# First norm: sums of squares on TensorE, first weights split in two pieces, a third projection tile run part by part

## The reference, cut to what matters

```python
def rmsnorm(x, g):
    return x * rsqrt(mean(x * x, axis=-1) + EPS) * g          # over 1024 channels

h = rmsnorm(x, norm_mix)                                      # x: 1024 positions x 1024 channels, float32
proj = h @ w_in + b_in                                        # 5 * 1024 columns
conv_val, conv_gate, pool_in, gate_a, gate_b = split(proj)    # 1024 columns each
u = causal_dwconv(conv_val * sigmoid(conv_gate), taps=31)     # then LayerNorm, silu, @ conv_w_out
...                                                           # pooled branch, gated merge, @ mix_w_out, + x
...                                                           # x = x + gdfn(rmsnorm(x)); final rmsnorm
```

## Time and profile before

| | |
|---|---|
| median of 3 runs | 1362.0 us (1360.88 to 1363.01) |
| the profiled execution | 1359.67 us |
| its span, first to last instruction | 1357.9 us |
| TensorE busy with matmuls | 1332.1 us (98% of the span) |
| DVE / POOL / ACT busy | 853.0 / 733.3 / 392.2 us |
| mean granted TensorE clock | 0.995 |

### The profile page before, as it was taken

How to read it: one execution, slowest core, us unless ns; L and a number is a source line. 1 busy time by engine, 2 the same in 40 slices (tenths; PEclk the granted TensorE clock), 3 DMA queues, 4 the chain that set the end, 5 groups by cost and what they waited for, 6 DMA issues and landing times.

```text
span 1357.9 us, 15759 instructions
## 1 busy us (share of the span) xinstructions
PE 1332.1 (98%) x6092; PEld 1108.4 (82%) x6092; DVE 853.0 (63%) x823; ACT 392.2 (29%) x555; POOL 733.3 (54%) x486
## 2 busy tenths in 40 slices
PE   7999999999999999999999999999999999999997
PEld 6888888888888788878887788888888888888887
DVE  6799999999997545545696455544554453320225
ACT  4311221211112441111245344343443433322210
POOL 5645536554453353356967887778777714434101
PEclk9999999999999999999999999999999999999999
DMA  5111111110111112344402222212221238531003
GB/s 195 63 49 58 34 47 47 47 47 31 47 53 42 46 47 78 121 133 147 141 31 93 93 93 87 79 68 93 94 78 68 103 118 315 188 109 62 0 1 124
DMA packets 32930, 114.47 MB, mean 84 GB/s; under 512 B 3040, under 2 KB 9184, under 8 KB 28768
## 3 DMA queue, kind: packets, MB, share of 16 engines
q1 hardware_dynamic: 29328, 104.12, 22.3%
q10 hardware_dynamic: 3536, 9.44, 1.9%
HBM read 93.62 MB, written 19.92 MB: 84 GB/s over the span
## 4 chain that ended last, share of the span: by engine, by line
PE 88%; DVE 4%; POOL 2%; issue 1%; ACT 1%; DVEq 0%; POOLq 0%; ACTq 0%
PE ps L1323 29%; PE ps L1325 29%; PE ps L1324 29%; DVE ga_r L1173 1%; DVE tmp L1081 1%; POOL h_lo L496 0%; POOL w_lo L541 0%; DVE res L1300 0%; PE ps L1377 0%; POOL h_lo L541 0%; PE ps L1387 0%; DVE raw L1179 0%; DVE res L1133 0%; DVE res L1166 0%; DVE res L1168 0%
## 5 line engine op out<-in xcount | busy, mean ns | idle before, releaser
L1323 PE MATMUL ps<-h_lo,w_hi 128*128 128x512 f32 (+1 forms) x972 | 374.9, 386 | 8.8 <-DVE h_lo L944 7.3
L1325 PE MATMUL ps<-h_hi,w_hi 128*128 128x512 f32 (+1 forms) x972 | 372.0, 383 | 0.0
L1324 PE MATMUL ps<-h_hi,w_lo 128*128 128x512 f32 (+1 forms) x972 | 372.0, 383 | 0.0
L1027 DVE SCALAR_TENSOR_TENSOR ps<-tmp,par,ps 128x1024 f32<-128x1024 f32 x224 | 267.7, 1280 | 0.0
L457 POOL TENSOR_SCALAR w_hi<-raw 128x1024 fp32r<-128x1024 f32 x66 | 71.6, 1085 | 309.7 <-issue 253.0
L1323 PEld LDWEIGHTS ps<-h_lo,w_hi 128*128 128x128 f32 x972 | 183.3, 189 | 46.9 <-DVE h_lo L944 8.7
L1324 PEld LDWEIGHTS ps<-h_hi,w_lo 128*128 128x128 f32 x972 | 183.3, 189 | 35.7 <-issue 0.5
L1325 PEld LDWEIGHTS ps<-h_hi,w_hi 128*128 128x128 f32 x972 | 183.2, 188 | 35.5
L1323 PE MATMUL ps<-ga_r,w_hi 128*128 128x512 f32 (+1 forms) x428 | 166.5, 389 | 3.4 <-POOL w_lo L541 2.4
L459 POOL TENSOR_TENSOR w_lo<-raw,w_hi 128x1024 fp32r<-128x1024 f32 x66 | 164.3, 2489 | 5.5
L1324 PE MATMUL ps<-cv_r,w_lo 128*128 128x512 f32 (+1 forms) x428 | 165.4, 386 | 0.0
(11 more groups left out here) (184 smaller groups left out, 1905.5 us busy)
## 6 DMA issues: line engine op xcount, KB each, us to landing
raw<-in_wstream SPq DMA_DIRECT2D x68, 512.0 KB, 3.5
tmp<-in_wffn SPq DMA_DIRECT2D x16, 1024.0 KB, 4.9
tmp<-g_kept SPq DMA_DIRECT2D x22, 512.0 KB, 4.3
res<-in_wffn SPq DMA_DIRECT2D x10, 1024.0 KB, 4.8
g_kept<-res SPq DMA_DIRECT2D x14, 512.0 KB, 2.6
raw<-in_wffn SPq DMA_DIRECT2D x5, 1024.0 KB, 4.9
res<-in_xT ACTq DMA_DIRECT2D x4, 1024.0 KB, 4.9
x_kept<-res ACTq DMA_DIRECT2D x16, 256.0 KB, 2.3
```

The costliest lines, as they stand in the source:

```text
L1027: dve.scalar_tensor_tensor(out=tile(cv, c) if last else acc, in0=glu(c, t), scalar=w, in1=acc, op0=ALU.mult, op1=ALU.add).then_inc(conv_la ...
L1323: nc.tensor.matmul(out, a_hi, b_lo, start=start, stop=False, skip_group_check=onto)
L1324: nc.tensor.matmul(out, a_lo, b_hi, start=False, stop=False, skip_group_check=onto)
L1325: return nc.tensor.matmul(out, a_hi, b_hi, start=False, stop=stop, skip_group_check=onto)
```

## The change

- **Sums.** The additions of parts 0 and 1 are gone (L980, L983, L993, and L505 of part 1). `variance1` of these parts now sums over the 8 squares as well: 16 matmuls in place of 2. In `variance` the wait for square i stands ahead of its first matmul, no longer all of them ahead of the first. `keep_busy(24)` becomes `keep_busy(14)`.
- **First weights.** POOL splits chunk 0 in two pieces of 512 columns. The high parts of chunk 1 and of chunk 2 are copied by ACT, in its queue behind the high half of tile 3 and of tile 6 of part 0; POOL subtracts for the low parts once they are there. The squares of part 1 on ACT now stand between the high halves of part 0, each behind one.
- **Third tile.** Chunk 2 (v1) has a home of its own (`third_raw`, loaded between the weights of chunk 1 and x of part 2), and goes into PSUM slot 2. TensorE's order is: v0 of part 0, the variance of part 1, g0 of part 0 with the broadcast of part 1 ahead of its tile 6, v1 of part 0; then for parts 1 to 3 the pair v0 and g0 with the variance of the next part ahead of tile 4, the broadcast of the next part, and v1. Scales and variances lie in banks 6 and 7.
- **Orders.** DVE inverts for part 1 after all of part 0 and for parts 2 and 3 behind value 6 of the part before. ACT's roots and squares move accordingly. POOL's queue after the low halves is glu0, then the split of chunk 3. The first convolution waits for both v0 and v1 to be read out.

```diff
-    SUMMED1 = 4
...
@@ SyncE
             load_weights(1)
+            sp.dma_start(third_raw, wstream[2 * P:3 * P, :]).then_inc(third_loaded, 16)
             load_x(2)
...
+            sp.wait_ge(w_split, 2)
+            sp.dma_start(raw[:, CH:2 * CH], wstream[3 * P:4 * P, :]).then_inc(raw_loaded[1], 16)
...
@@ GpSimd
-            for n in range(2):
-                split(n, n, 0)
+            pool.wait_ge(raw_loaded[0], 16)
+            for a, hi_done, lo_done in ((0, first_hi, first_lo), (CH // 2, w_hi_done, w_split)):
+                r, hi, lo = (t[:, a:a + CH // 2] for t in (raw, w_hi, w_lo))
+                pool.tensor_scalar(hi, r, 1.0, 0.0, ALU.mult, ALU.add).then_inc(hi_done, 1)
+                pool.wait_ge(hi_done, 1)
+                pool.tensor_tensor(lo, r, hi.bitcast(f32), ALU.subtract).then_inc(lo_done, 1)
+            for n, (r, hi, lo) in ((1, [t[:, CH:2 * CH] for t in (raw, w_hi, w_lo)]), (2, (third_raw, third_hi, third_lo))):
+                pool.wait_ge(w_hi_done, n + 1)
+                pool.tensor_tensor(lo, r, hi.bitcast(f32), ALU.subtract).then_inc(w_split, 1)
...
-            for p in range(1, PARTS):
+            for p in range(2, PARTS):
...
             for n in range(2, 2 * LOOSE):
-                split(n, n % 2, n // 2)
+                if n > 2:
+                    split(n, n % 2, n // 2)
@@ ScalarE
+            deviation1(0)
             for k in range(KT):
+                high1(0, k)
                 square1(1, k)
+                if k == 3:
+                    act.wait_ge(raw_loaded[1], 16)
+                    act.wait_ge(w_hi_done, 1)
+                    act.activation(w_hi[:, CH:2 * CH], raw[:, CH:2 * CH], ACT.Copy).then_inc(w_hi_done, 1)
+                if k == 6:
+                    act.wait_ge(third_loaded, 16)
+                    act.activation(third_hi, third_raw, ACT.Copy).then_inc(w_hi_done, 1)
+            deviation1(1)
+            for k in range(KT):
+                square1(2, k)
+            for k in range(KT):
+                high1(1, k)
+                square1(3, k)
+                if k == 5:
+                    deviation1(2)
...
@@ VectorE
             invert1(0)
-            for k in range(1, SUMMED1):
-                ...
             for p in range(PARTS):
...
-                       None if p + 1 == PARTS else 7 if p == 0 else 4, lambda: invert1(p + 1))
+                       6 if 0 < p < PARTS - 1 else None, lambda: invert1(p + 1))
+                if p == 0:
+                    invert1(1)
...
+            dve.wait_ge(val_out, 2)
             conv(0)
@@ TensorE
-            keep_busy(24)
+            keep_busy(14)
             variance1(0)
             keep_busy(3)
             broadcast1(0)
             keep_busy(3)
-            for p in range(PARTS):
+            pe.wait_ge(first_lo, 1)
+            one_part(0, slot(0), w_hi[:, 0:CH], w_lo[:, 0:CH], low_of(n1[0], False), {KT // 2: lambda: pe.wait_ge(w_split, 1)})
+            pe.wait_ge(w_split, 2)
+            one_part(0, slot(1), w_hi[:, CH:2 * CH], w_lo[:, CH:2 * CH], None, {0: lambda: variance1(1), KT - 2: lambda: broadcast1(1)})
+            pe.wait_ge(w_split, 3)
+            one_part(0, slot(2), third_hi, third_lo)
+            for p in range(1, PARTS):
                 between = {}
                 if p + 1 < PARTS:
-                    between[6 if p == 0 else 1] = lambda: variance1(p + 1)
-                    if p:
-                        between[4] = lambda: broadcast1(p + 1)
+                    between[KT // 2] = lambda: variance1(p + 1)
                 pair_part(0, 0, *part(p), low_of(n1[p], p >= 2), w_used if p + 1 == PARTS else None,
                           s1_half if p == 1 else None, between)
-                if p == 0:
-                    broadcast1(1)
+                if p + 1 < PARTS:
+                    broadcast1(p + 1)
+                last = one_part(p, slot(2), third_hi, third_lo)
+            last.then_inc(w_used, 1)
...
-            for kind, i in START[2:]:
+            for kind, i in START[3:]:
```

More of the change, by code:

```diff
@@ L263, in build @@
         n1_nt = [[cv[:, i * PART:(i + 1) * PART] for i in range(n, n + 4)] for n in (8, 12)]
+        third_hi, third_lo, third_raw = ga_r[:, 0:CH], ga_r[:, CH:2 * CH], ga[:, 4 * SEQ:4 * SEQ + CH]
+        n1_scale = [bank(6 + p % 2, 0, PART) for p in range(PARTS)]
+        n1_var = [bank(6 + p % 2, PART, PART + PART // P) for p in range(PARTS)]
         n1_diag = [cv[:, i * PART:(i + 1) * PART] for i in range(16, 16 + PARTS)]
@@ L302, in build @@
         n1 = [norm(p, ("sq_a", "val", "hi", "lo_v") + extra)
-              for p, extra in enumerate((("sum", "sq_v"), ("sum",)) + (PARTS - 2) * (("sum", "lo_p"),))]
+              for p, extra in enumerate((("sq_v",), ()) + (PARTS - 2) * (("sum", "lo_p"),))]
         pads, sums, pw_hi_done, pw_lo_done, p_mean, p_hi, p_lo = sems(
@@ L497, in low_halves @@
                                        ALU.subtract).then_inc(z["lo_p"], 1)
-            for p in range(1, PARTS):
+            for p in range(2, PARTS):
                 z, squares = n1[p], n1_sq[p % 2]
-                for k in range(SUMMED1 if p == 1 else 1, KT):
+                for k in range(1, KT):
                     pool.wait_ge(z["sq_a"], k + 1)
@@ L605, in _, with deviation1, high1 @@
                 square1(0, k)
-            deviation(n1[0], 0, bank(6), PART // P)
+            def deviation1(p):
+                deviation(n1[p], 4 * p, n1_var[p], PART // P)
+            def high1(p, k):
+                act.wait_ge(n1[p]["val"], k + 1)
+                act.activation(tile(h_hi, k, *part(p)), n1_nt[p % 2][k % 4], ACT.Copy).then_inc(n1[p]["hi"], 1)
+            deviation1(0)
             for k in range(KT):
+                high1(0, k)
                 square1(1, k)
-            for p in range(PARTS):
-                for k in range(KT):
[L611 to L619, removed]
+                if k == 3:
[13 more added lines that the diff above has]
+                    deviation1(2)
+            for p in (2, 3):
+                for k in range(KT):
+                    high1(p, k)
+                    if p == 2 and k == 5:
+                        deviation1(3)
             def hold(i):
@@ L644, in value @@
                 wait(act, cv_done, c - 1)
-                act.activation(glu(c, PAD), slot(0), ACT.Identity, bias=par1("b_in", c)).then_inc(val_out, 1)
+                act.activation(glu(c, PAD), slot(2 if c == 1 else 0), ACT.Identity, bias=par1("b_in", c)).then_inc(val_out, 1)
             def gate(c, turn, n):
@@ L1398, in variance1 @@
             def variance1(p):
-                squares = n1_sq[p % 2]
-                variance(bank(6 + p % 2), [((n1[p]["sum"], 5 if p == 0 else KT - 1), squares[0])], var_done, PART // P)
+                squares, z = n1_sq[p % 2], n1[p]
+                if p >= 2:
+                    variance(n1_var[p], [((z["sum"], KT - 1), squares[0])], var_done, PART // P)
+                else:
+                    variance(n1_var[p], [((z["sq_v"], k // 2 + 1) if p == 0 and k % 2 else
+                                          (z["sq_a"], k // 2 + 1 if p == 0 else k + 1), squares[k]) for k in range(KT)],
+                             var_done, PART // P)
             def broadcast1(p):
@@ L1410, in keep_busy, with one_part @@
                     nc.tensor.matmul(bank(0, 0, P), ones[:, :], ident[:, :], start=True, stop=True)
-            keep_busy(24)
+            def one_part(p, out, a_hi, a_lo, ready=None, between={}):
+                a, b = part(p)
+                for k in range(KT):
+                    if k in between:
+                        between[k]()
+                    if ready:
+                        pe.wait_ge(*ready(k))
+                    last = three(out[:, a:b], a_hi[:, k * P:(k + 1) * P], a_lo[:, k * P:(k + 1) * P],
+                                 tile(h_hi, k, a, b), tile(h_lo, k, a, b), k == 0, k == KT - 1)
+                return last
+            keep_busy(14)
             variance1(0)
```

32 lines of the change are left out of this document (9 added, 23 removed).

## The result

| | before | after |
|---|---|---|
| median of the runs, us | 1361.44 (1360.48 to 1363.01) | 1377.78 (1376.84 to 1377.89) |
| ratio | | 1.0117, 95% interval 1.01 to 1.0135 |
| profiled execution / its span, us | 1359.67 / 1357.9 | 1377.72 / 1375.9 |
| granted clock, mean | | 0.985 |

The change makes the kernel slower by 1.2%, 16.3 us between the medians and 18.0 between the spans of the two profiled executions. That of the kernel before, 1359.67 us, is faster than all four that were timed beside the changed kernel, so some of the 18.0 belongs to the execution and not to the change. The forecast was 1369, 1363 to 1373: the direction was right, and the forecast slowdown of 7.0 us is less than half of what came.

The account below looks back on a forecast made before the run. Prediction: TensorE's pace bounds the kernel. Its start, matmuls, stalls, variances and broadcasts put g1 at 70.9 against 63.9, 7.0 us later; 1359.67 + 7.0 = 1366.7 profiled, 1369 as median, the median of before lying 2.3 higher; range 1363 to 1373.

Parts of the forecast that it names:

- Start: Kernel start up to TensorE's v0: variance 1 us late, but first value at 13.7, v0 at 15.15, 2.8 us earlier.
- The rival of a cheap variance: Variances of parts 0 and 1 at the 25 ns floor: 2.8 us off part 1's, total 1365.5; chance 7%.
- POOL holds DVE: Part 0: DVE's low halves 4 and 7 wait for POOL's subtractions, done at 20.7 and 25.5.
- POOL doesn't hold DVE: Rival, part 0: low half 4 at 17.3, low 7 at about 22; 5.5 us less, 1363.5; chance 10%.
- fills the holes: Rival: third tile fills TensorE's stalls, DVE never held; 1.5 us earlier, 1360.5, or 1356 with chunk 3 ready; chance 11%.
- The variance of part 1: Behind v0 of part 0, on TensorE's path with nothing beside it: 3.6 us, to 29.5.
- the rival of a clock drop: Drop of 3.4 us at 25.5, half on part 1's variance: 1.6 us more, 1370.6; chance 15%.
- a drop at 20 would lie in a stall and cost nothing: Remark on part 0: a clock drop at 20 us falls where TensorE stalls anyway, so costs nothing.
- Part 1's stall: Ahead of tile 6 in part 1, TensorE idles 1.8 us for DVE's value 7 and low half 6.
- g1's idle time: Ahead of g1, first whole tile both kernels run alike: TensorE idles 4.6 us for POOL's split of chunk 3.
- Convolutions: DVE's first starts at 68.2 less 0.4, 11.5 later; 4.5 later against TensorE, inside the 5.9 of room, costing nothing.
- both drops at once: Case little above the forecast, named with the range of 1363 to 1373; no chance of its own given.

Follow-up runs that it names:

- e1: Changed kernel with the variances of parts 0 and 1 taken with 128 moving columns in place of 1: 1371.77 us, ratio 1.0091 to the kernel before.
- e2: Changed kernel with ten constant matmuls in each of part 0's two stalls, ahead of tiles 4 and 7: 1373.9 us, ratio 1.0107 to the kernel before.
- e3: Changed kernel with ACT's copies of chunks 1 and 2 both behind high half 7 of part 0: 1373.23 us, ratio 1.0093 to the kernel before.
- e7: Changed kernel with POOL's two subtractions for chunks 1 and 2 each cut into four pieces of 256 columns: 1373.22 us, ratio 1.0091.
- e6: Changed kernel with 128-column variances in parts 0 and 1 and ten constant matmuls in each of part 0's two stalls: 1369.56 us, ratio 1.0069.
- e4: Changed kernel with own tiles for chunk 3, split by POOL behind the sums of part 3, long before glu 0: 1373.67 us, ratio 1.0101.
- e9: e8 with ACT's copies for the first pooled map behind g2's reading, their low parts behind chunk 9's split: 1369.47 us, ratio 1.006 to the kernel before.
- e5: Changed kernel with part 1's one-column variance in two-matmul pieces in the stalls of v0, not behind it: 1373.48 us, ratio 1.0093.
- e8: Changed kernel with moved chunk copies, subtractions in pieces, wide variance in instalments, earlier broadcasts and own tiles for chunk 3: 1360.66 us, ratio 1.0007.

## Why the prediction was wrong, step by step

*Start.* Right. keep_busy ended at 7.9 (7.5), the variance at 11.6 (11.3), the first value came at 14.09 (13.7), TensorE's v0 at 15.63 (15.15). The price of a variance matmul from its weight load, 0.112 us, holds: 3.81 us for 32 is 0.119, and e1 shows that the columns don't enter. The rival of a cheap variance is out. What the sum had no term for is that the start differs between executions: the same 28 instructions of keep_busy end at 7.88 in after and at 6.51 in e2. From 5 to 6 us 6 instructions go by in the one and 11 in the other, the paces of the two clock levels, though the granted clock reads 1.00 for both there.
The Trainium skill ("TensorE: Matmul & The Clock Gate", section "LDWEIGHTS (loading the stationary operand)") gives a load about P/1.2 ns for P columns; for 128 that is an estimated 107 ns, and 3.4 us for 32. The trace is near it at the full clock (0.119 us each) and not at the low one (6.82 us for 32, 0.213 each); the floor of 25 ns, weighed in the prediction, did not bind here.

*POOL holds DVE.* Right, in place and size: low half 4 done at 21.0 (20.7), low 7 at 25.8 (25.5). e3 and e7 confirm the cause. Hence the rivals "POOL doesn't hold DVE" and "fills the holes" are out.

*The variance of part 1, and the rival of a clock drop.* Here it failed: the sum priced the variance of part 1 at 3.6 us and all that surrounds it at full clock. The rival had the mechanism, at 15%, and the wrong size: "a drop as long as that one, 3.4 us by its matmul spacing, at 25.5 would lie on the variance: half of it, 1.6 us". I took one drop of fixed length, like the one behind the idle time ahead of 17.99. What came was a drop at 21.4 that lasted 17 us, and the one-column variance that lies in it does not bring the clock back: it went on for 5.2 us of wide matmuls behind it, while in e1, with 128 columns, it ended inside the variance. The slow price stood in the prediction as a bound, 0.213, and 32 x 0.213 = 6.8 is what the variance took; the bound was not carried into the range.

The drop's cost, by the rows of after against those of e6: 1.3 us ahead of the variance (26.67 against 25.41), 3.1 on it (6.82 against 3.73) and 1.7 on g0's tiles 0 to 5 (18 matmuls at 0.213 in place of 0.12); together 6.1, the difference at g1 (what tile 6 and the broadcast lose besides, part 1's stall gives back: 0.52 against 1.09). Of the 1.3, 0.95 is there at v0's first tile (15.63 against 14.68). It comes in part from the low stretch of 11.2 to 14.6, where the broadcast takes 1.08 in place of 0.70, and in part, at most 0.8, from keep_busy, which ended 0.76 later in that execution.

The drop behind g1's idle time, 76.0 to 82.9, was not in the sum at all, though the row that showed such a drop was at hand: half of the 6.1 us from g1's start to its end, 3.1, of which e6, whose stretch there is half as long, leaves 1.7. The prediction's own remark, "a drop at 20 would lie in a stall and cost nothing", was true of the first 3.4 us and for that reason misleading.

*Part 1's stall.* The 1.8 us ahead of tile 6 became 0.52: TensorE was itself late by the clock, and DVE had the time. The forecast's stall was partly paid by the loss I had left out. But e6 shows 1.09 and not 1.8 as well, and in both runs the 0.8 of part 2 is 0.26 and the 0.9 of part 3 is not in the list of waits. As e6's g1 agrees with the forecast all the same, other small terms were short by about as much; no run separates them.

*g1's idle time.* Right: 4.6 forecast, 4.45 measured, released by POOL's w_lo. e4 shows that it is worth 4.1 us in the end, its low stretch included, since a later wait of 2.7 us and its low stretch take part of it.

*Convolutions.* Right that they cost nothing: 5.9 us between sum and mean, before and after. The first starts at 73.54, 5.7 later than the forecast 67.8, about what g1 is late by (5.9); that v1's reading would end earlier than glu 0 was wrong, by 0.2 us. The last sum slips 15.8, as TensorE does. The forecast took the 5.9 us for room and its slip of 4.5 for what is used of it; none of it was used, since the sum ends with POOL's subtraction, which moves with TensorE (413.58 before, 429.38 after). That the distance hangs on the order of POOL's queue, e9 shows.

*Sum.* +7.0 forecast at g1, +12.9 measured, +6.8 in e6 without low clock. At the end e6 still has 9.4 us more span than before; of the 2.6 us behind its g1, 1.7 are the low stretch there and 0.9 are open; they lie behind the mean (935.9 us from there to the end, against 934.9). In the changed kernel 5.9 us were lost ahead of g1, 2.9 between g1 and the mean, and 2.2 behind the mean, where the low stretch from 465.2 to 468.6 accounts for 1.7. It follows the 16 one-column matmuls of the next variance (462.77, 1.95 us); e2, e3, e5 and e7 show such a stretch there too, but before, e1, e4, e6, e8 and e9 have the same 16 matmuls and none, and what decides it was not settled. It may be the execution: those of the kernel before differ in mean clock from 0.989 to 0.996, and the profiled one has 0.995. That e6's time, 1369.56, is the forecast's 1369 is therefore partly luck: the sum lacked the 1.7.

*The range.* It reached 1373, "both drops at once". With the measured costs of the drops the same rival gives 1366.7 + 6.1 + 3.1 + 2.3 = 1378.2. (A slip in the chances: "a third and a bit" of 11% is 4%, not 0.07; the range doesn't hang on it.)

## What to carry to other kernels

Before work is moved onto TensorE between stalls, look at what that work gives the array to do: a run of one-column matmuls is 100% busy in the profile, and yet every run here in which it followed a stall stayed at the 1.2 GHz level for another 3.0 (e3) to 5.4 us (e5) of wide matmuls. Widening the moving side to the width of the weights cost no time here (3.74 against 3.81 us for 32), so try it wherever PSUM has room; widths between 1 and 128 were not tried. And when a wait of TensorE goes, ask which engines meet at other moments because of it: in e9 a wait of 2.7 us went, by a new order of ACT's and POOL's work; DVE's additions and POOL's subtractions met more often, and the kernel lost 7 to 9 us in all. Which of the two did it, the wait or the order, e9 does not separate.

## What the runs showed of the hardware

- One-column matmuls with 128-column weights: full clock if it was full before (3.63 us for 32), and then the clock falls, inside the run or shortly behind it, with no idle time: at 28.8 in e2, where they ran from 24.42 to 28.05, and at 11.2 after, where they ran from 7.88 to 11.56. With 128 columns it doesn't (e1 behind its first variance, e6 behind both). If the clock was low, they don't raise it (21.4 to 38.5 after); with 128 columns it rose during them (29.3 in e1). Runs of 16 such matmuls were followed by a fall in some runs and not in others.
- A DVE subtraction of two SBUF operands waits until the running POOL instruction, a subtraction too, ends: 2.37 us beside one of 1024 columns, 0.75 and 0.87 beside pieces of 256, 0.42 alone. The values, with the scale in PSUM, aren't held (0.47 beside the pieces). The pieces cost POOL something: beside DVE's work the four took 3.35 and 2.97 us in place of 2.35 and 2.34, and yet the last low half came 3.1 us earlier.
